# A packed first weight tile, products of ones ahead of the first loads, and a norm's sum moved into a matmul tile

## The reference, cut to what matters

```python
xn = rmsnorm(h, lw['norm_mix'])          # h * rsqrt(mean(h*h) + eps) * gain
proj = xn @ lw['w_in']                   # 1024 -> 4368 columns
z, xbc, dt, gate, xl = jnp.split(proj, [s1, s2, s3, s4], axis=-1)
xl, lru_buf_new = causal_conv(xl, lru_buf, lw['conv_lru_w'], lw['conv_lru_b'])
```

## Time and profile before

| | us |
|---|---|
| median of 3 runs | 1776.24 (1776.1 to 2847.4) |
| the profiled execution, its own time | 1774.02 |
| span of the profile | 1772.0 |
| TensorE matmul busy | 1721.9 |
| VectorE busy | 1508.3 |
| ScalarE busy | 849.9 |
| GpSimd busy | 561.5 |

### The profile page before, as it was taken

One profiled execution on the slowest core, in us unless ns is written; L12 is line 12 of the kernel. 1 busy time (PEld: TensorE's weight loads), 2 busy tenths in 40 slices (PEclk: granted clock), 3 DMA queues, 4 the chain that ended last, 5 costly groups with the idle time before them and its releaser, 6 DMA issues. The chain is left out here.

```text
span 1772.0 us, 29786 instructions
## 1 busy us (share of the span) xinstructions
PE 1721.9 (97%) x11375; PEld 1693.5 (96%) x11375; DVE 1508.3 (85%) x2722; ACT 849.9 (48%) x1238; POOL 561.5 (32%) x420
## 2 busy tenths in 40 slices
PE   7999998999999999999999999999999999999996
PEld 6999997889999999999999999999999999999996
DVE  7747999988678789999999999878889878899887
ACT  5556652434333333357777777523333332333276
POOL 3100220000000012345444444455456645566400
PEclk9999999999999999999999999999999999999998
DMA  4212343244345557799999999999999999999611
GB/s 159 95 60 84 136 137 109 66 169 151 127 135 160 180 172 236 261 321 354 377 361 367 348 359 376 400 389 398 396 396 397 396 399 396 397 395 393 244 60 51
DMA packets 164588, 461.12 MB, mean 260 GB/s; under 512 B 17152, under 2 KB 77504, under 8 KB 161760
## 3 DMA queue, kind: packets, MB, share of 16 engines
q1 hardware_dynamic: 118368, 291.43, 45.5%
q0 software_dynamic: 46080, 167.79, 25.2%
HBM read 404.61 MB, written 54.56 MB: 259 GB/s over the span
## 5 line engine op out<-in xcount | busy, mean ns | idle before, releaser
L171 ACT CAST Rh<-Rw 128x1024 fp32r<-128x1024 f32 x272 | 284.5, 1047 | 346.2 <-DMA Rw<-vn 304.7
L176 DVE TENSOR_TENSOR Rl<-Rw,Rh 128x1024 fp32r<-128x1024 f32 x272 | 332.0, 1221 | 96.9 <-ACT Rh L171 96.2
L1593 POOL DMA_INDIRECT ug<-un,idxU x160 | 242.8, 1517 | 520.4 <-DVE dots L2057 334.9
L1647 PE MATMUL PS<-Hh,Rh 128*128 128x384 f32 x1024 | 343.7, 336 | 8.9 <-DVE Hl L2049 5.8
L1634 PE MATMUL PS<-Xh,Rh 128*128 128x384 f32 x992 | 342.7, 345 | 3.8 <-DVE Rl L176 2.8
L1649 PE MATMUL PS<-Hh,Rl 128*128 128x384 f32 x1024 | 342.2, 334 | 0.0
L1648 PE MATMUL PS<-Hl,Rh 128*128 128x384 f32 x1024 | 342.1, 334 | 0.0
L1593 POOL DMA_INDIRECT ug<-vn,idxU x160 | 271.7, 1698 | 207.8 <-DVE yacc L2062 164.5
L1635 PE MATMUL PS<-Xl,Rh 128*128 128x384 f32 x992 | 334.2, 337 | 0.0
L1636 PE MATMUL PS<-Xh,Rl 128*128 128x384 f32 x992 | 333.3, 336 | 0.0
L1647 PEld LDWEIGHTS PS<-Hh,Rh 128*128 128x128 f32 x1024 | 192.2, 188 | 12.1 <-issue 7.0
(11 more groups left out here) (446 smaller groups left out, 3051.2 us busy)
## 6 DMA issues: line engine op xcount, KB each, us to landing
Rw<-uw SPq DMA_DIRECT2D x144, 512.0 KB
Rw<-vn SPq DMA_DIRECT2D x128, 512.0 KB
Wr<-wm SPq DMA_DIRECT2D x51, 512.0 KB, 3.3
gates<-stg SPq DMA_DIRECT2D x12, 2048.0 KB
acts<-Ab SPq DMA_DIRECT2D x124, 192.0 KB
Aq<-acts SPq DMA_DIRECT2D x31, 768.0 KB, 15.7
Gq<-gates SPq DMA_DIRECT2D x30, 768.0 KB
L<-acsd SPq DMA_DIRECT2D x4, 1024.0 KB, 8.7
```

The lines of the kernel that those rows point to most:

```text
L171: a.copy(self.Rh[:, q, :], self.Rw[:, q, :]).then_inc(self.S("rhi"), 1)
L176: v.tensor_tensor(self.Rl[:, q, :], self.Rw[:, q, :], self.Rh[:, q, :].bitcast(F32), ALU.subtract).then_inc(self.S("rlo"), 1)
L1593: p.indirect_dma_start(out=ug[:, r % 4, :], out_offset=None, in_=un if r < IDC else vn, in_offset=bass.IndirectOffsetOnAxis(ap=idxU[:, r % ...
L1647: pe.matmul(out, Rh[:, q, w], hh, start=(g == 0), stop=False)
```

## The change

Three parts, all ahead of or in the first three tiles:

- **Tile 0 packed.** The host lays the 8 slices of 16 columns side by side in one slice of 128 columns. The load, the high part and the low part of tile 0 take that one slice; `tile(0)` takes its weights from it, still 16 columns in each matmul.
- **Products of ones.** TensorE, once `ones` has been written, runs 20 float32 matmuls of `ones` (128x128) by `ones` (128 columns) into a bank that tile 2 writes later from scratch.
- **The sum inside tile 2.** The two matmuls on `sqz` stand behind slice k = 2 of tile 2, not ahead of tile 2. `hi(2)` stands behind the fourth square, not the sixth; `lo(2)` behind the fourth addition, not the sixth.

```diff
+WARM = 20
 # sync
-            sp.dma_start(Wr[:, n % 2, :, :], wm[n, :, :, :]).then_inc(S("wf%d" % (n % 2)), 16)
+            w = slice(0, ND * NH // P) if n == 0 else slice(0, ND)
+            sp.dma_start(Wr[:, n % 2, w, :], wm[n, :, w, :]).then_inc(S("wf%d" % (n % 2)), 16)
 # tensor
+        def squares():
+            pe.wait_ge(S("const"), 2)
+            pe.wait_ge(S("sqz"), ND - 1)
+            for q in range(2):
+                m = pe.matmul(pair(3)[:, q, :], ones[:, :], sqz[:, q * HT:(q + 1) * HT], start=True, stop=True)
+            m.then_inc(S("sq_free"), ND)
+                wt = w_sb[:, s, k, :] if n else w_sb[:, 0, k * NH // P, k * NH % P:k * NH % P + NH]
                     for q in range(2):
-                        r = pe.matmul(pair(b, m)[:, q, :], w_sb[:, s, k, 0:m], x_sb[:, k, q * HT:(q + 1) * HT],
+                        r = pe.matmul(pair(b, m)[:, q, :], wt, x_sb[:, k, q * HT:(q + 1) * HT],
                                       start=first, stop=last)
+                if n == 2 and k == 2:
+                    squares()
+        pe.wait_ge(S("const"), 1)
+        for i in range(WARM):
+            pe.matmul(PS[:, 0, 0:P], ones[:, :], ones[:, :], start=True, stop=True)
         for n in range(NW):
-            if n == 2:
-                pe.wait_ge(S("const"), 2)
-                pe.wait_ge(S("sqz"), ND - 1)
-                for q in range(2):
-                    m = pe.matmul(pair(3)[:, q, :], ones[:, :], sqz[:, q * HT:(q + 1) * HT], start=True, stop=True)
-                m.then_inc(S("sq_free"), ND)
             tile(n)
 # scalar
-            a.copy(Whi[:, s, :, :], Wr[:, s, :, :]).then_inc(S("whi"), 1)
+            w = slice(0, ND * NH // P) if n == 0 else slice(0, ND)
+            a.copy(Whi[:, s, w, :], Wr[:, s, w, :]).then_inc(S("whi"), 1)
-            if k == 5:
+            if k == 3:
                 hi(2)
 # vector
-            v.tensor_tensor(Wlo[:, s, :, :], Wr[:, s, :, :], Whi[:, s, :, :].bitcast(F32), ALU.subtract
+            w = slice(0, ND * NH // P) if n == 0 else slice(0, ND)
+            v.tensor_tensor(Wlo[:, s, w, :], Wr[:, s, w, :], Whi[:, s, w, :].bitcast(F32), ALU.subtract
                             ).then_inc(S("wlo"), 1)
-            if k == 6:
+            if k == 4:
                 lo(2)
 # layout on the host
-    wm[0, :, :, 0:NH] = w[:, s2:s3].reshape(ND, P, NH).transpose(1, 0, 2)
+    wm[0].reshape(P, ND * P)[:, 0:ND * NH] = w[:, s2:s3].reshape(ND, P, NH).transpose(1, 0, 2).reshape(P, ND * NH)
```

## The result

The changed kernel takes 1778.51 us (median of 20 runs), the kernel before 1775.74: a ratio of 1.0014, 95% interval [1.0007, 1.0020], so 1.2 to 3.6 us slower. That is within 2%, slower by a hair, and inside the forecast's range; the forecast had +1.1 us. The profiled execution took 1779.33 us with a span of 1777.3, 5.3 us above the span of the kernel before; single executions of one kernel lie some microseconds apart, so the two profiles differ by more than the medians do.

A forecast was written before the change was run, and what follows sets the result against it. TensorE, busy 1721.9 of 1772.0 us, was taken as the bound, with the norm's reciprocal holding tile 3 at the start. -0.5 (chain) + 1.6 (slow stretch) = +1.1 us on 1776.24 gave 1777.3 us; range 1773.5 to 1780.

The forecast's parts named there:

- What bounds the start: First tiles: the norm's reciprocal and what hangs on it hold tile 3; tile 4's start, 38.19, carries the shift.
- Part 1: Packed tile 0: h lands 1.10 us earlier (bounds 0 and 1.10); tile 1 starts at 14.45, not 16.98.
- The norm's chain: From sum through root, reciprocal, dts and lo(3) to tile 3: each 0.5 us earlier, tile 3 at 31.57.
- the queue was full: DMA at 418 GB/s between 4.5 and 9.7 us, the reason for taking the upper bound of 1.10 us.
- Part 2: Ahead of tile 0: products of ones end between 5.4 and 9.7; tile 0 starts at 8.1 at full clock.
- Part 3: Tile 2 starts 3.6 us earlier, sum at 22.8; the wait ahead of tile 3 grows to about 4.0 us.
- The clock: It falls in the wait ahead of tile 3, costing that tile 1.7 us, bounds 0 and 2.7.
- my sum: At tile 4: -0.5 us from the norm's chain, +1.6 from the slow stretch past lo(4), together +1.1 us.
- The clock stays up: Rival, chance 0.20: no clock fall in the wait ahead of tile 3; only -0.5 us is left, 1775.7.
- The win of TensorE stays: Rival, chance 0.07: the reciprocal doesn't hold tile 3, and all 3.6 us won reach the end, 1772.6.
- The products of ones don't lift the clock: Rival, chance 0.05: ahead of tile 0 they hold TensorE without raising the clock; +5.6 to +7.2 us, about 1783.
- The packed load brings nothing: Rival, chance 0.13: h lands no earlier, being bound by latency, not bytes; +2.2 us with the clock's 1.6, 1778.4.

The follow-up runs named there:

- ones_only: Kernel before with only the 20 products of ones ahead of tile 0 added; ratio to before 1.0009, on a second measurement 1.0003.
- sum_only: Kernel before with only the sum moved behind slice 2 of tile 2 and the earlier hi(2) and lo(2); ratio to before 1.0013.
- late_pack: short_pack with the way of dts through DRAM behind load(5), ScalarE's and VectorE's work on it one tile later; ratio to before 0.9991, 1773.72 us.
- no_ones: Changed kernel without the products of ones, packing and moved sum kept; ratio to before 1.0005.
- short_pack: Kernel before with tile 0 packed, hi(3) and lo(3) ahead of root and reciprocal, dts behind the reading of tile 1; ratio to before 0.9991.
- changed_again: The changed kernel measured a second time, nothing altered; ratio to before 1.0012.
- load2_held: Changed kernel with load(2) held back on SyncE until all of h has landed; ratio to before 1.0011.
- fill_wait: Changed kernel with 16 more products of ones behind tile 2, in the wait ahead of tile 3; ratio to before 1.0006.
- short_all: Changed kernel with hi(3), lo(3) ahead of root and reciprocal, dts behind the reading of tile 1, sum behind slice 1 of tile 2; ratio to before 1.0009.

## Why the prediction was right, and where its sizes were off

**What bounds the start: right.** The reciprocal and what hangs on it hold tile 3. ones_only shows it from one side (tile 1 1.4 us earlier, tile 3 not), sum_only from the other (tile 1 not later, sum later, tile 3 later), late_pack by taking it away.

**Part 1: right in kind, wrong in size.** I took the upper bound, 1.10 us; the high part of slice 4 starts at 10.19, 0.44 us earlier than in the earlier trace rows. Over the profiles it started at 10.47 to 10.63 in the four with the wide tile 0 and at 9.57 to 10.37 in the nine packed ones that hold nothing back, about 0.6 us apart in their means. So tile 1 came at 15.12, not 14.45, and all behind it was 0.6 us later than forecast: the sum 23.5, not 22.8. The norm's chain did not move by -0.5 but by +0.15. Part of the miss is "the queue was full": I read the 418 GB/s from 4.5 us on, but the wide load of tile 0 had landed by 5.31, so much of what the packing takes away moved ahead of that stretch. Between 3.0 and 4.5 us the DMA moved 335 GB/s in the kernel before and 238 in the changed one (330 to 357 in all four wide kernels, 202 to 253 in all ten packed ones). That is 0.15 MB less, some 0.35 us at 418 GB/s by an estimate from these rows; the rest of the missing 0.66 us stays open.

**Part 2: right.** The products end at 7.3 (forecast 5.4 to 9.7, taken 8.1) and tile 0 starts at full pace as soon as its data are there (8.07, forecast 8.1).

**Part 3: right.** 3.86 us of wait against about 4.0 forecast; both of its ends came about 0.6 us later than forecast.

**The clock: right, and mis-sized.** The term that was most off is the 1.7 us, taken from the tile at 330.78, whose slow stretch was 3.4 us long. Tile 3 took 41.08 - 32.20 = 8.88 us against 6.02, so 2.9 us lost, 0.2 us beyond what I had as the upper bound. The price of a fall is not one number: the slow stretches here were 3.4 us long (sum_only, no_ones, short_pack) or over 6 us (changed, changed_again, load2_held). Put together: +0.15 (the chain) + 2.86 (tile 3) - 0.1 (the wait of tile 4 for its weights, which the kernel before had) = +2.9 at tile 4 and 2.8 at the B row; my sum had -0.5 + 1.6. The medians differ by 2.8 too, but that the sizes agree so well is partly luck: the second measurement of the changed kernel gave 1.0012, some 2.1 us, and one profile stands for each B row.

**The number.** 1778.51 against the forecast 1777.3 looks closer than it was: the change was missed by 1.7 us, and the median of the kernel before, over more runs, came 0.5 us lower than the one I started from. The range was 6.5 us wide, over twice the effect, so the rows above bear the argument and not the time.

The Trainium skill (TensorE: Matmul & The Clock Gate, "HAM oscillation — how this bites in real kernels") describes a kernel whose matmul bursts start at the low clock because of the wait ahead of each. The two stretches of the changed kernel and of fill_wait agree: 0.50 after an idle wait, 1.00 after a filled one. In sum_only and no_ones the burst behind the same wait started at full pace and fell to the low clock 0.5 to 0.7 us later.

**The rivals.** "The clock stays up" is out in five profiles of five with this wait. "The win of TensorE stays" is out by ones_only. "The products of ones don't lift the clock" is out by tile 0's pace. "The packed load brings nothing" is out by half: it brings 0.4 to 0.6 us of the 1.10.

**What stays open: the experts' turn.** The wait there is 1.9 to 2.7 us in the six profiles without the products of ones and 2.2 to 5.7 in the eight with them, over 3.7 in six. In the changed kernel VectorE waits there for gathered rows:

```profile
1140.29 1.22 DVE L2068 CUSTOM_DVE_ANT_0 ug<-ug,xtok 128x1024 f32<-128x1024 f32 x1 [3.06 <-DMA ug<-un,idxU]
```

Here a gathered row lands late and the low part of the second product's operand (L2060, at 1145.07) stands behind it on VectorE. Why 20 matmuls in the first 8 us should make a gather late at 1140 us I can't say; fill_wait and load2_held have the ones and a short wait, so it is a tendency of fourteen single executions and not shown as a cause. It would explain why short_all and ones_only were slower than their first 208 us, and why the time of no_ones came out below the changed kernel's. A loss of the changed kernel's size doesn't need it, since sum_only, without ones and with a turn of 1.9 us, loses as much (1.0013). How much of the changed kernel's own 2.8 us comes from the start and how much from this turn is open.

Later falls of the clock stay open in the same way. TensorE's wait of 2.19 us ahead of the row at 277.45 of the kernel before is in all fourteen profiles to the hundredth. In seven of them the granted clock over the next 4.5 us is 1.00, in the other seven, the two of the changed kernel among them, it is 0.62 to 0.64, and 24 to 26 matmuls run where 37 did. So the B row does not carry to the end unchanged.

## What to carry to other kernels

Before making an engine's first work faster, follow the chain to the first place where it waits already: what is won ahead of that place only lengthens the wait, unless the chain that ends the wait is shortened too. A longer wait of TensorE is not free even off the path, because the matmuls behind it may run at half pace; here 2.3 us more of waiting cost 2.9, and in two other kernels with the same wait 1.6. And a sum that a long chain hangs on should be issued as soon as its operand is ready, not behind matmuls that nobody waits for.

## What was not expected of the hardware

The same wait of 3.86 or 3.87 us, with the same work behind it, was followed by two different prices. In the profiles of changed, changed_again and load2_held the granted clock fell while TensorE was still idle, tile 3 ran at the 1.2 GHz level for about 6 us from its first matmul and took 8.88 us in changed and 8.83 in load2_held. In sum_only and no_ones it was still 1.00 for the first 0.5 to 0.7 us of tile 3, fell only then and rose again 3.4 us later; tile 3 took 7.64 us. And the wait of 2.19 us was followed by a lower clock in seven of the fourteen profiles. What a wait costs is thus read from several executions, not one.

The column of the granted clock reads 1.00 in the first microseconds of the kernel before, where 24 matmuls run at half pace: at the start the pace is to be trusted, not the column.
